# Low halves of the weights written over the raw units, two buffers a slot instead of three

## The reference, cut to what matters

```python
def first_block(...):
    for l in range(2):
        proj = rms_norm(h) @ w_in[l]                 # 2048 x 4176, split in nine parts
        mix  = concat(diff_attention, dsa_attention, chunk_spatial_gating)
        h = h + rms_norm(mix @ w_out[l])
        h = h + rms_norm(memory_attention(rms_norm(h), rms_norm(mem)))
        h = h + rms_norm(silu(n @ gate) * (n @ up) @ down)   # hidden 5632
def second_block(...):
    proj = rms_norm(x) @ w_in                        # q k v, gates, u, z
    y_a = (sliding_window_attention * silu(gate)) @ w_attn_proj
    y_s = (glu(gelu(s5_ssm(u))) * silu(z)) @ w_ssm_proj
    return x + (sigmoid(g_a) * y_a + sigmoid(g_s) * y_s) @ w_out
```

## Time and profile before

| | before |
|---|---|
| median of 3 runs | 3211.94 us (3208.05 to 3216.03) |
| profiled execution: its time, its span | 3211.86 us, 3210.0 us |
| mean granted TensorE clock | 0.989 |
| busy: PE, DVE, ACT, POOL | 3084.4, 2001.6, 1508.7, 58.6 us |
| chain of work that ended last | PE 82%, DVE 7%, ACT 3%, issue 3%, DMA 1% |
| loads of raw units | 1032 of 512.0 KB, median 3.7 us from issue to landing |

### The profile page before, as it was taken

How to read it: one execution, slowest core, us unless ns; L and a number is a source line. 1 busy time by engine, 2 the same in 40 slices (tenths; PEclk the granted TensorE clock), 3 DMA queues, 4 the chain that set the end, 5 groups by cost and what they waited for, 6 DMA issues and landing times.

```text
span 3210.0 us, 44795 instructions
## 1 busy us (share of the span) xinstructions
PE 3084.4 (96%) x16254; PEld 2652.1 (83%) x16254; DVE 2001.6 (62%) x2322; ACT 1508.7 (47%) x1970; POOL 58.6 (2%) x100
## 2 busy tenths in 40 slices
PE   8999898999999999899898999999998998999999
PEld 7899777888888887898787888888887887888987
DVE  6567756555555555676656665565656567887664
ACT  5545445444444444545455455555544453333543
POOL 0000000000000000000000000000000100000000
PEclk9999999999999999999999999999999999999999
DMA  7654453655555555544554655665554534554555
GB/s 283 219 166 164 144 186 132 217 191 192 192 186 190 192 190 176 178 171 138 177 174 148 217 205 201 216 205 205 204 201 152 179 106 171 194 194 163 182 184 170
DMA packets 168368, 590.39 MB, mean 184 GB/s; under 512 B 26093, under 2 KB 26281, under 8 KB 165801
## 3 DMA queue, kind: packets, MB, share of 16 engines
q1 hardware_dynamic: 150784, 545.33, 49.7%
q10 hardware_dynamic: 14968, 28.47, 2.6%
q0 software_dynamic: 2480, 14.73, 1.3%
HBM read 574.81 MB, written 15.99 MB: 184 GB/s over the span
## 4 chain that ended last, share of the span: by engine, by line
PE 82%; DVE 7%; ACT 3%; issue 3%; DVEq 2%; DMA 1%; POOL 1%; POOLq 0%; ACTq 0%; SPq 0%
PE acc L661 21%; PE acc L663 21%; PE acc L662 21%; PE acc L669 4%; PE acc L671 4%; PE acc L672 4%; DVE lo L1622 2%; PE tp L680 1%; PE tp L713 1%; ACT hi L1087 1%; DVE sr L2295 1%; PE tp L1029 1%; DMA raw<-in_stream 1%; PE tp L1018 1%; ACT lg L1169 0%
## 5 line engine op out<-in xcount | busy, mean ns | idle before, releaser
L1622 DVE TENSOR_TENSOR lo<-raw,hi 128x1024 fp32r<-128x1024 f32 x1032 | 1244.0, 1213 | 901.0 <-ACT hi L1087 892.0
L1087 ACT ACTIVATE hi<-raw 128x1024 fp32r<-128x1024 f32 x1032 | 1078.5, 1050 | 1268.3 <-PE acc L663 1009.6
L661 PE MATMUL acc<-hi,xh 128*128 128x512 f32 (+2 forms) x2528 | 984.6, 389 | 21.7 <-DVE lo L1622 16.8
L663 PE MATMUL acc<-hi,xl 128*128 128x512 f32 (+2 forms) x2528 | 973.9, 385 | 0.0
L662 PE MATMUL acc<-lo,xh 128*128 128x512 f32 (+2 forms) x2528 | 973.4, 385 | 0.0
L661 PEld LDWEIGHTS acc<-hi,xh 128*128 128x128 f32 x2528 | 475.7, 188 | 121.1 <-DVE lo L1622 16.3
L663 PEld LDWEIGHTS acc<-hi,xl 128*128 128x128 f32 x2528 | 475.4, 188 | 94.8
L662 PEld LDWEIGHTS acc<-lo,xh 128*128 128x128 f32 x2528 | 475.9, 188 | 91.2
L669 PE MATMUL acc<-xh,hi 128*128 128x256 f32 x1152 | 338.2, 294 | 14.4 <-DVE lo L1622 9.3
L671 PE MATMUL acc<-xl,hi 128*128 128x256 f32 x1152 | 330.3, 287 | 0.0
L672 PE MATMUL acc<-xh,lo 128*128 128x256 f32 x1152 | 329.9, 286 | 0.0
(11 more groups left out here) (374 smaller groups left out, 2451.4 us busy)
## 6 DMA issues: line engine op xcount, KB each, us to landing
raw<-in_stream SPq DMA_DIRECT2D x1032, 512.0 KB, 3.7
turn_scratch<-made ACTq DMA_DIRECT2D x8, 1024.0 KB, 6.8
gpost<-in_post_g POOLq DMA_DIRECT2D x6, 1024.0 KB, 4.9
rotc<-turn_scratch ACTq DMA_DIRECT2D x8, 512.0 KB, 4.5
rots<-turn_scratch ACTq DMA_DIRECT2D x8, 512.0 KB, 6.3
bpad<-in_b_pad ACTq DMA_DIRECT2D x8, 512.0 KB, 8.1
toep_scratch<-toep_scratch POOLq DMA_DIRECT2D x1, 2286.0 KB, 16.2
y<-in_mem SPq DMA_DIRECT2D x4, 512.0 KB, 8.1
```

The source lines that it names most:

```text
L661: nc.tensor.matmul(o, ah, high, start=first, stop=False)
L663: last = nc.tensor.matmul(o, al, high, start=False, stop=final)
L1087: nc.scalar.activation(hi[s][:, :, 0:w], raw[s][:, :, 0:w], ACT.Copy).then_inc(hi_done, 1)
L1622: nc.vector.tensor_tensor(lo[s][:, :, 0:w], raw[s][:, :, 0:w], hi[s][:, :, 0:w].bitcast(F32), ALU.subtract).then_inc(split_done, 1)
```

## The change

The low half is no longer a buffer of its own: `lo[s]` is given the address of `raw[s]`, so DVE's subtraction at line 1622 writes over its own first operand. A slot has then two buffers of 8 KB a partition, not three. A raw unit can't be loaded into the slot until PE has used the low half that lies there, so SP waits for `unit_used` where it waited for `split_done`. The 32 KB a partition that come free are not used; the buffers behind lie lower.

```diff
         raw = [sb(f"raw{s}", [P, KU, W]) for s in range(SLOTS)]
         hi = [sb(f"hi{s}", [P, KU, W], F32R) for s in range(SLOTS)]
-        lo = [sb(f"lo{s}", [P, KU, W], F32R) for s in range(SLOTS)]
+        lo = [at_offset(f"lo{s}", place[0] - 2 * SLOTS * KU * W * 4 + s * KU * W * 4, [P, KU, W], F32R) for s in range(SLOTS)]
...
-                sp.wait_ge(split_done, s + 1)
+                sp.wait_ge(unit_used, s + 1)
                 sp.dma_start(flat(raw[s]), stream[s * P:(s + 1) * P, :]).then_inc(raw_loaded[s], 16)
             with sp.Fori(1, (MU + L * LU + SU) // SLOTS) as i:
                 for s in range(SLOTS):
-                    sp.wait_ge(split_done, i * SLOTS + (s + 1))
+                    sp.wait_ge(unit_used, i * SLOTS + (s + 1))
                     sp.dma_start(flat(raw[s]), stream[bass.ds((i * SLOTS + s) * P, P), :]).then_inc(raw_loaded[s], 16)
```

## The result

The kernel after takes 3387.63 us (median of 4 runs, 3384.17 to 3391.39), the kernel before beside it 3211.30 us (4 runs, 3208.05 to 3216.03): ratio 1.0548, 95% interval 1.053 to 1.0566. It is slower, as forecast, but by 176 us and not by 72, and the time lies above the range of 3240 to 3345. The kernel before was measured again beside the experiments, on several chips, and its median lay between 3211.3 and 3216.8 us; so a difference between two experiments is good to about 5 us. The profiled execution took 3384.17 us with a span of 3382.3 us and a mean granted clock of 0.975 (before 0.989).

The account below looks back on a forecast made before the run. PE, busy for 96% of the span, was taken to bound the kernel; terms of 4, 15, 10, 8, 10 and 24 us sum to 71, plus 1 for the start, giving 3284 us from 3211.9, range 3240 to 3345.

Parts of the forecast that it names:

- term 1: Feed-forward loop: splits fit, only the second layer's few worst landings delay the add of down; 4 us (0 to 20).
- Rival B: The lead left hides the later load; chance 0.12 with some loss (3222 to 3250 us), 0.08 with none.
- rival D: Faster: loads stop queuing behind ACT's scan loads, PE's 10.3 us wait for lo goes; 3202 us, chance 0.03.
- Rival C: The loop becomes bound by the slot's round if landings settle above 4.3 us; above 3345 us, chance 0.05.
- the cost has to be summed by places: Whole kernel: each place with less than 3.4 to 4.4 us of lead loses time; the places sum to 71 us.
- term 2: Narrow groups, ckv and the 256-column groups before qk2: late splits and copies cost 7.6 us a layer, 15 (8 to 22).
- term 5: Attention steps of the b heads and second block: 0.5 us each, 10 us with its head rows (0 to 25).
- Term 3: Norms: quarters 2 and 3 of xh stand behind a late hi; 1.5 us for each of 7, 10 us (0 to 18).
- term 4: Start and end of each feed-forward: blocks of DVE work no longer fit the lead; four places, 8 us (2 to 12).
- term 6: Scan: late lo makes PE wait 3.0 us in each of 8 chunks; 24 us (10 to 32).

Follow-up runs that it names:

- the wait alone: Kernel before with only SP's wait changed to unit_used, lo kept in its own buffer: 3386.78 us, ratio 1.0532.
- all six kernels: The change, its wait without the overlay, three changed orders of ACT and DVE work, and the change with filler transposes: 3387.63, 3386.78, 3374.24, 3358.24, 3346.77, 3391.84 us.
- the ring at u-8: Against the kernel before: 8 in-place raw/lo buffers and 4 of hi, a load issued when PE has used the unit 8 before: 3205.55 us, ratio 0.9966.
- with fillers: The ring at u-8 plus 48 transposes on PE before the first norm's wait and 28 before the others: 3205.51 us, ratio 0.9965 to the kernel before.
- u-5: Same 8 in-place and 4 hi buffers, load issued when PE has used the unit 5 before: 3233.84 us, ratio 1.0054 to the kernel before.
- u-6: Same 8 in-place and 4 hi buffers, load issued when PE has used the unit 6 before: 3205.16 us, ratio 0.9963 to the kernel before.

## Why the prediction was right about the direction and wrong about the size

**The mechanism stood.** SP waits for PE, hi for the load, the lead shrinks by what was forecast, the loop keeps its pace (term 1: 4 forecast, 2.9 measured), lo keeps its 1.21 us, and the wait alone gives the whole cost. Rival B (the lead left hides it) and rival D (faster) are out. Rival C had the right side of the range and the wrong cause: the loop that it would slow down is not slower, and landings are not longer. Whether ACT's own loads gain from fewer raw loads in flight no run here isolates. The Trainium skill (DMA: Bandwidth & Descriptors, Anatomy of one DMA) gives 3.2 us for 512 KB as an estimate. Its fit is for transfers issued by GpSimd, which the text on record leaves out, and SP issues the loads here. The 3.2 of the first layer's loop agrees all the same, and the loads of the second layer's loop still have a median of 4.1 us (2110 to 2510 us). By the skill's figure the forecast would have been lower still, so the error is not in the landing.

**What failed is the count and size of the places** in the step "the cost has to be summed by places". Terms 2 to 6 came out 1.7 to 3.2 times too small, by three errors.

- *Read-outs were priced only in the feed-forward loop and behind `ckv`.* Term 1 asked whether the add of down, behind a split, is in time for PE's next need of the PSUM buffer. In the short groups before qk2 that same question was given "about 2 us" a layer, without a row. There some groups keep PE for only 1.4 us (`uv1`, `uk1`), so a buffer is wanted back after less work, while the split in front of the copy is as late as anywhere. ACT in the kernel after at such a place, and the matmul of PE that needs the buffer:

```profile
211.70 1.06 ACT L1087 ACTIVATE hi<-raw 128x1024 fp32r<-128x1024 f32 x1 [3.90 <-DMA raw<-in_stream]
214.34 1.06 ACT L1087 ACTIVATE hi<-raw 128x1024 fp32r<-128x1024 f32 x1 [1.58 <-DMA raw<-in_stream]
215.30 1.01 ACT L1096 ACTIVATE QI<-acc 128x1024 f32<-128x1024 f32 x1
...
216.36 0.39 PE L669 MATMUL acc<-xh,hi 128*128 128x256 f32 x1 [2.69 <-ACT QI L1096]
```

  ACT sits idle 3.90 and then 1.58 us for two loads, only then copies QI out, and PE has waited 2.69 us when the copy ends at 216.31. The short groups cost 16.0 us in both layers where 4 were forecast. The other 21.7 of term 2's 37.8 are in `qk1` and `qk2` (8.9 and 12.8), the wide groups behind them. Of these, 11 are the same question once more: the first product of `qk1` and `qk2` waits for the copy of QI or qbT out of a short group's buffer, as in the lines above. 2.5 are waits for steps of lg, which belong to term 5's b heads, and 8 are longer busy time. In all, the waits for QI, QA, qbT, kbT and kaT grew by 24.0 us: the step that failed most is this one, priced at 4. That the late splits in front of the copies hold them up is read from such rows, as no run changed the order there. For ckv with the unit behind it the sum held (11.2 forecast, 10.3 measured with qk0), though 3.1 of it is busy time.

- *Chains through several engines.* Term 3 priced two quarters of each norm but not the output norm ahead of it, which makes h: PE's wait for h (line 713) grew by 15.8 us, and the order that reads a group out before the last split takes just that back. At the ends of the feed-forwards (term 4) and in attention (term 5) there were 0.5 to 2 us a place without a row behind each, and both came out 2.5 to 3 times that. In the scan the waits were forecast nearly right in sum (24, measured 27.0), but in part by luck: 17.8 of them are for lo, as term 6 had it, and the rest for DVE's uT (5.2) and ACT's load of bpad (3.9), which it did not name.

- *No term for busy time.* PE's busy time grew by 55.7 us. From the clock records, time at the half clock (1.2 and not 2.4 GHz) went from 71.7 to 167.3 us. 95.6 us at half speed do the work of 47.8, so this accounts for most of the growth. In the scan 13.7 us of busy time came on top of the waits. Without these 55.7 us the sum would be 117.

**What stays open.** How much of the 55.7 us is a cost of its own. At the norms it is none: a faster PE there waits longer. From `qi0` to `cu` and in the scan behind `ag1` the change spends 61.5 us at half clock and the kernel before 23.9; at 0.45 us each that is 17 us, an estimate. For `ag1`, at half clock for 13.7 us in all six kernels, no pair of runs tells. In the ring at u-8, where PE waits less, the scan takes 351.8 us with 23.9 at half clock and 350.6 with 10.2 (with fillers), so there little of it costs. Nor did I run the short groups by themselves; what the text says of them rests on the rows above.

## What to carry to other kernels

A buffer that is freed by the consumer and not by the producer takes its transfer out of the lead. Before such a change, ask how far ahead the load is released and compare that with landing plus the steps to the consumer; here one unit more (u-5) brought back 154 of 182 us, and two (u-6) all of it. When a producer's engine works in fixed order, a late split delays what is written behind it, so price the read-outs and chains at the shortest group, not in the widest loop, and take one measured place as the size for its kind only if the kinds are alike. And before a run with a changed order is read, see in its trace that the order did change where it was meant to. Memory saved by an overlay can be spent on distance: 8 in-place buffers and 4 of hi in the place of 12 took away the whole cost of 5.5%, and the 0.35% gained beyond that came at the start.

## What the runs showed of the hardware

- A subtraction that writes over its first operand costs the same: 1214 against 1213 ns at 128x1024.
- The landing of the same 512 KB load has two levels, 3.2 and 4.2 us, and which one a stretch has changes from kernel to kernel. In the first layer's loop it is 3.2 us before and after. In the second layer's loop it is 4.2 us before, 4.1 after, and 3.2 in the ring released at u-8 (2100 to 2400 us). Over all loads the median fell from 3.7 us to 3.3 in every kernel that waits for `unit_used`. What sets the level stays open.
- More time at the full clock bought nothing where PE waits afterwards: 51 us less at the half clock, 0 us gained (0.9966 and 0.9965). In `qk1` it did buy time: 34.0 us at full clock, 35.5 with 3.4 us of it at the half, at the same wait for QI.
